# Attention's first loads in order of use, and the last stage's first operands loaded during attention

## What is computed

```python
proj = h @ w_in                                     # q, k, v, latent, indexer and gate columns
y_a = swa_sink_attention(qa, ka, va, sinks) @ w_o_a  # attention output: 512 columns per branch
y_b = dsa_mla_attention(qb, c_kv, qi, k_idx, w_idx, w_uk, w_uv, topk) @ w_o_b
mix = (sigmoid(g_a) * y_a + sigmoid(g_b) * y_b) @ w_out
h = layer_norm(ALPHA * h + mix, ln1_g, ln1_b)
ff = (silu(h @ w_ff_gate) * (h @ w_ff_up)) @ w_ff_down
return layer_norm(ALPHA * h + ff, ln2_g, ln2_b)
```

## Time and profile before

| | |
|---|---|
| three executions | 3710.90, 3723.59, 3720.97 us |
| their median | 3720.97 us |
| the profiled execution | 3723.26 us, its span 3721.0 us |
| granted PE clock, mean over the span | 0.979 of full |
| PE busy | 3484.1 us of the span (94%) |
| stages by first and last PE instruction | up to 1049.5; attention 1052.8 to 1990.2; last stage 2008.4 to the end |
| mean rate of the transfers | 126 GB/s |

### The profile page before, as it was taken

The page is one execution under the profiler, slowest core; times in us unless marked ns, Lnnn a source line. Parts: engine busy times, 40 slices in busy tenths (PEclk is TensorE's granted clock), DMA queues, the critical chain, the costliest instruction groups (busy, mean ns, idle before and its releaser), DMA issues. The chain is left out here.

```text
span 3721.0 us, 52571 instructions
## 1 busy us (share of the span) xinstructions
PE 3484.1 (94%) x17924; PEld 2896.5 (78%) x17924; DVE 2220.3 (60%) x3097; ACT 1923.8 (52%) x3592; POOL 1698.7 (46%) x1806
## 2 busy tenths in 40 slices
PE   6888999898989999999997998999999999999997
PEld 5776777677767888988996777778887888888786
DVE  5236888787623565666543665764556545555867
ACT  3223787788635798887553332343334333344443
POOL 5233443765311222222003665656665666554756
PEclk9999999999989999999998999999999999999998
DMA  8344323332221111100005445754545444365663
GB/s 272 129 125 109 101 88 124 124 89 74 83 70 51 40 42 35 35 16 19 23 11 181 152 167 180 242 188 141 183 142 188 160 142 150 123 249 191 235 227 132
DMA packets 338458, 468.44 MB, mean 126 GB/s; under 512 B 23184, under 2 KB 225120, under 8 KB 334992
## 3 DMA queue, kind: packets, MB, share of 16 engines
q1 hardware_dynamic: 310064, 387.47, 32.1%
q10 hardware_dynamic: 28128, 77.60, 5.7%
HBM read 311.21 MB, written 153.78 MB: 125 GB/s over the span
## 5 line engine op out<-in xcount | busy, mean ns | idle before, releaser
L2610 POOL TENSOR_TENSOR ff_rounded_ring<-ff_raw,ff_rounded_ring 128x512 fp32r<-128x512 f32 x264 | 383.4, 1464 | 292.0 <-ACT ff_rounded_ring L2757 289.4
L100 PE MATMUL ff_bank<-ff_rounded_pair,ff_rounded_ring 128*128 128x512 f32 x1232 | 482.9, 392 | 16.0 <-POOL ff_rounded_ring L2610 10.9
L101 PE MATMUL ff_bank<-ff_rounded_pair,ff_rounded_ring 128*128 128x512 f32 x1232 | 481.8, 391 | 0.0
L102 PE MATMUL ff_bank<-ff_rounded_pair,ff_rounded_ring 128*128 128x512 f32 x1232 | 481.6, 391 | 0.0
L1777 PE MATMUL at_ctx<-at_p_t,at_c_nat 128*128 128x128 f32 (+1 forms) x2432 | 344.5, 282 | 8.3 <-ACT at_ctx_t L1893 7.3
L1777 PEld LDWEIGHTS at_ctx<-at_p_t,at_c_nat 128*128 128x128 f32 (+1 forms) x2432 | 301.2, 191 | 35.6 <-ACT at_ctx_t L1893 13.2
L1887 ACT ACTIVATE at_p_t<-at_turn 128x512 f32<-128x512 f32 (+4 forms) x416 | 213.2, 544 | 204.9 <-PE at_turn L1754 174.9
L2615 POOL TENSOR_TENSOR ff_rounded_ring<-ff_raw,ff_rounded_ring 128x512 fp32r<-128x512 f32 x154 | 211.4, 1378 | 175.9 <-ACT ff_rounded_ring L2807 175.9
L3038 DVE TENSOR_TENSOR ff_rounded_a_ring<-ff_f_q,ff_rounded_a_ring 128x512 fp32r<-128x512 f32 x154 | 211.0, 1380 | 129.9 <-ACT ff_rounded_a_ring L2799 128.7
L100 PEld LDWEIGHTS ff_bank<-ff_rounded_pair,ff_rounded_ring 128*128 128x128 f32 x1232 | 232.7, 189 | 68.2 <-POOL ff_rounded_ring L2610 13.8
L102 PEld LDWEIGHTS ff_bank<-ff_rounded_pair,ff_rounded_ring 128*128 128x128 f32 x1232 | 232.7, 189 | 48.9
(11 more groups left out here) (401 smaller groups left out, 9075.5 us busy)
## 6 DMA issues: line engine op xcount, KB each, us to landing
f_kept<-ff_resid SPq DMA_DIRECT2D x154, 256.0 KB, 2.7
ff_f_q<-f_kept ACTq DMA_DIRECT2D x12, 2816.0 KB, 10.7
pj_raw<-in_w_in SPq DMA_DIRECT2D x58, 512.0 KB, 4.5
proj<-se_row SPq DMA_DIRECT2D x104, 256.0 KB, 2.2
ff_raw<-in_w_ff_gate SPq DMA_DIRECT2D x22, 1024.0 KB, 10.9
ff_raw<-in_w_ff_up SPq DMA_DIRECT2D x22, 1024.0 KB, 6.3
ff_raw<-down_comb SPq DMA_DIRECT2D x88, 256.0 KB, 2.7
ff_raw<-in_w_ff_down SPq DMA_DIRECT2D x66, 256.0 KB, 3.3
```

Of the source, the lines that this page charges most:

```text
L100: pe.matmul(out, lhs_lo, rhs_hi, start=start, stop=False, skip_group_check=goes_on)
L101: pe.matmul(out, lhs_hi, rhs_hi, start=False, stop=False, skip_group_check=goes_on)
L102: return pe.matmul(out, lhs_hi, rhs_lo, start=False, stop=stop, skip_group_check=goes_on)
L2610: pool.tensor_tensor(ring[:, step % RING, 1, :].rearrange("p (k c) -> p k c", c=P), f_operand(it, q, m), f32(ring[:, step % RING, 0, :]).r ...
```

## The change

It has three parts.

1. **Attention's list of loads (SP) is put in order of use.** Behind `qb` come the first keys, the distances of tile 0, the first three 128-row pieces of `c_nat` (`load_natural`), the distances of tile 1, the four small operands, the first window's operands, and then `wuv`, the other keys and the rest of `c_nat`. `c_nat` gets semaphores of its own (`nat_loaded`), waited for where PE first multiplies with it (step 0 and step 16), so that the logits wait for `c_hi` and `c_lo` alone. PE's wait for `w_loaded` moves from ahead of step 0 into step 1.
2. **Early loads.** Two buffers of 16 KB a partition, `early[0]` and `early[1]`, are placed at the far end of the memory, above a pad of 32 bytes. While attention runs, SP loads columns 0 to 511 of `w_o_a` and `w_o_b` into the first (behind the loads of tile 6) and the first branch's half of group 0's attention output into the upper half of the second (behind those of tile 7, with a wait for the stores of the first four tiles). The four `p_t` buffers of attention, which stood among its others, now lie in the other half of `early[1]`.
3. **The last stage uses them.** `w_o` is now held as two buffers by column (`early[0]`: columns 0 to 511; `w_o_second`: 512 to 1023) with both branches' rows in each, so rounding and subtracting a block take one instruction of 128x1024 each. `att` is `early[1]`. SP starts with the gates, then loads the second half of `w_o`; ACT loads only the second half of the first group's attention output. `ring` and `a_ring` lie where `early[0]` and `early[1]` were, two of three `raw_f` buffers lie in `att`, and the first two loads of feed-forward weights wait for `att_lo_ready` instead of the last block of `w_o`.

Every buffer of attention but `p_t` stands 8192 bytes lower than before and every one of the last stage but those named 16384 bytes lower or elsewhere by a multiple of 256. `early[0]`, `early[1]` (and so `p_t`, `att`, `ring`, `a_ring`) begin at a byte that leaves 192 when divided by 256; their predecessors began at one that leaves 128. The built program has 32 ACT and 32 POOL instructions of computation fewer, two waits of PE fewer, the same matmuls and the same DVE instructions.

```diff
+    def far(self, name, shape, dt=F32):
+        return self.enter_context(self.nc.sbuf_tensor(f"{self.tag}_{name}", shape, dt, side="right"))
...
-        p_t = [s.sb(f"p_t{u}", [P, 4, P]) for u in range(PT)]
+        p_t = [early[1][:, KT // 2 + u, :].rearrange("p (m c) -> p m c", m=4) for u in range(PT)]
...
+                first, first_rows = width(1), -(-width(1) // P)
+                load_keys(0, first, 0)
                 load_distances(0)
+                load_natural(0, first_rows, 0)
                 load_distances(1)
...
                 load_window(0)
                 load_values(0)
+                sp.dma_start(wuv[:, :, :], w_uv[0].rearrange("h r d -> r h d")).then_inc(w_loaded, 16)
+                load_keys(first, L, 1)
+                load_natural(first_rows, TILES, 1)
...
                     load_values(t + 1)
+                    if t == 5:
+                        for e, src in enumerate((w_o_a, w_o_b)):
+                            sp.dma_start(early[0][:, 4 * e:4 * e + 4, :], src.rearrange("(k p) c -> p k c", p=P)[:, :, 0:GROUP]).then_inc(early_loaded[0], 16)
+                    if t == 6:
+                        sp.wait_ge(attn_stored, 32 * TPG)
+                        sp.dma_start(early[1][:, 0:4, :], attn[0:512, 0:GROUP].rearrange("(k p) c -> p k c", p=P)).then_inc(early_loaded[1], 16)
...
-                        pe.wait_ge(c_loaded[t // 2], (64, 32)[t // 2])
+                        pe.wait_ge(c_loaded[t // 2], 32)
...
+                        if n in (0, 2 * HEADS):
+                            pe.wait_ge(nat_loaded[n // (2 * HEADS)], (16, 32)[n // (2 * HEADS)])
...
-                pe.wait_ge(w_loaded, 16 * 5)
                 for n in range(STEPS):
...
+                    if n == 1:
+                        pe.wait_ge(w_loaded, 16 * 5)
...
+        ring, a_ring = [s.far(name, [P, RING, 2, GROUP], F32R) for name in ("ring", "a_ring")]
...
+        raw_f = [att[:, 4 * u:4 * u + 4, :].rearrange("p k c -> p (k c)").rearrange("p (k c) -> p k c", c=2 * P) for u in range(2)]
...
-                        for u in range(2):
-                            sp.wait_ge(lo_ready[u], use1(NG - 1, KT - 2 + u) + 1)
+                        sp.wait_ge(att_lo_ready, KT * NG)
...
-                load_w_o(0)
                 load_gates(0, 0)
                 load_gates(0, 1)
+                load_w_o(0)
                 load_w_o(1)
...
-                load_w_o(2)
-                load_w_o(3)
...
-                        for d, src in block_parts(b):
-                            last = pool.tensor_tensor(as_k(w_lo[u])[:, d, :], src, as_k(f32(w_hi[u]))[:, d, :], ALU.subtract)
-                        last.then_inc(lo_ready[u], 1)
+                        pool.tensor_tensor(as_k(w_lo[u]), block_part(b), as_k(f32(w_hi[u])), ALU.subtract).then_inc(lo_ready[u], 1)
...
-                        if g == 0:
-                            act.wait_ge(w_o_loaded[b // 2], 32)
+                        if g == 0 and b < 4:
+                            act.wait_ge(early_loaded[0], 32)
+                        elif g == 0:
+                            act.wait_ge(w_o_loaded[b // 2 - 2], 32)
...
-                    for e in range(2):
+                    for e in range(0 if g else 1, 2):
                         act.dma_start(att[:, 4 * e:4 * e + 4, :], ...
...
+            kept.far("pad", [P, KT])
+            early = [first.far(f"half{u}", [P, KT, GROUP]) for u in range(2)]
```

77 lines of the change are left out of this document (37 added, 40 removed).

## The result

| | before | after |
|---|---|---|
| executions | 6: 3710.90 to 3723.59 us | 6: 3729.64 to 3746.27 us |
| median | 3716.72 us | 3740.11 us |
| profiled execution, its span | 3723.26, 3721.0 us | 3741.65, 3739.9 us |
| granted PE clock | 0.979 | 0.979 |

The ratio is 1.0065, with a 95% interval of 1.0053 to 1.0076: the kernel became slower by 23 us where 16 us of gain were forecast, and its time lies above the range of 3695 to 3715 us. Both savings that the forecast counted are there at their own places; two losses that it set at 0 are larger than both together.

What follows compares the result with a forecast made beforehand. PE was taken as the bound, busy 94% of the span, so only its waits at two stage starts could pay. Terms of -6.5 and -9.5 us, 16.0 off the 3721.0 us median, gave 3705 us, range 3695 to 3715.

Steps and rivals of the forecast that it cites:

- The start of attention: Up to step 0's transposes: waits for first keys and distances go, the clock stays full; -6.5 us, bounds -4.0 and -7.1.
- I take the upper end: At attention's start: PE stays at 2.4 GHz, with no idle stretch since its warm-up; 2.5 us saved, bounds 0 and 2.5.
- The clock falls elsewhere: Rival: a half-clock stretch like 1086 to 1096 comes once more (3710 us, chance 0.14) or vanishes (3700 us, 0.09).
- The loads during attention: Attention: three added 1 MB transfers make nobody wait; cost 0, without the slack up to 2 x 11.6 us once.
- The start of the last stage: PE's first product there comes 10.6 us sooner, 1.0 us is given back; -9.5 us, bounds -6.0 and -10.6.
- 32 ACT and 32 POOL instructions fewer lie beside a busy PE: 0: Rest of the last stage: fewer ACT and POOL instructions change nothing, as PE is busy there; 0 us.
- The addresses: I take 0 for it: `ring` and `a_ring` beginning 64 bytes past a multiple of 128 cost nothing, judged by transposes from `u_b`; 0 us.
- Slower: Rival: new places of `ring` and `a_ring` slow the products reading them; 3755 us at 4%; chance 0.05 beyond 2.2%.
- the signs for both starts: No waits 1063 to 1070, full clock 1070 to 1076, transposes near 1069.2; last stage's only PE wait 7 to 9 us.
- unchanged rows for L100 to L102: Sign of being right: these product rows stay as before; an L100 median above 395 ns would show it wrong.
- The last of the wrong signs: A start of either stage is sooner but the span's end is not: a later load or the clock took it back.

Runs made afterwards that it cites:

- e8: The kernel before with only attention's first loads put in order of use, with their own semaphores and waits; 3708.81 us, ratio to before 0.9996.
- e2: The changed kernel with POOL's subtraction of a block in two instructions of 128x512 instead of one; 3722.19 us, ratio to before 1.0025.
- e9: The changed kernel with a pad of 96 bytes and POOL's subtraction in four instructions of 128x256; 3696.6 us, ratio to before 0.9955.
- e6: The changed kernel with the last stage's near-side buffers, the pairs (moving operands) among them, moved by 64 bytes; 3716.76 us, ratio to before 1.0002.
- e1: The changed kernel with a pad of 96 bytes instead of 32, so far-end buffers begin at multiples of 128; 3716.48 us, ratio to before 1.001.
- e5: The changed kernel with a pad of 96 bytes and POOL's subtraction in two instructions of 128x512; 3699.61 us, ratio to before 0.9959.
- e13: e5 with attention's first loads in the order of the kernel before; 3700.95 us, ratio to before 0.9961.

## Why the prediction was wrong

- **The start of attention** (-6.5): right at its place, -7.4 in the profile. As a gain in the whole it was too much: 3.0 us in the mean of the traces, 1.6 in e8's time. The 4.0 us of waits are there (PE's idle time in attention is 3.8 us less in the mean, and less in every trace). The step that failed is "I take the upper end" of the clock's saving, 2.5 us: it is there from 1059 to 1063, but over the whole of attention PE's busy time scatters by 10 us with the granted clock, and nothing of it can be seen. The rival "The clock falls elsewhere" described this.
- **The loads during attention** (0): right, +0.4 us over 918.
- **The start of the last stage** (-9.5): right. PE starts 10.1 us sooner where 10.6 were worked out, and gives back 1.1 us in its wait for the second slice where 1.0 was taken. For `att`'s second half ACT waited 1.9 us, PE not at all.
- **"32 ACT and 32 POOL instructions fewer lie beside a busy PE: 0"** failed: +18 us. I counted the instructions that went, and not that the 32 left are twice as long. The row on which I rested, 82.6 of 83 us busy, ends at 2100, just where the first of the places with an idle PE begins: the window from 2098 shows 26.34 of 28 us. I had also cited the rule at issue, on the Trainium skill's page "SBUF — State Buffer", section "Who interferes with whom" (a VectorE instruction that needs the pair of ports shared with GpSimd waits for GpSimd's whole instruction), and applied it to two slices at the stage's start. The trace of the kernel before had the case to which it applied nine times in twelve: its scaling took 1284 ns at the least, for the first of each group, and 2305 in the median. With one POOL instruction twice as long, the scaling would wait for 2.4 us less POOL's head start instead of 1.3 us less it, 1.1 us more: 3.4 us, as measured. Twelve scalings took 16.4 us more of DVE's time (3 x 2.15 for the first of each group, which had been alone before, and 9 x 1.11). On PE, which is what counts, the trace of e2 is 18.5 us shorter here: 10.4 us less idle (22.5 against 32.9) and 8.1 less busy with the same matmuls (372.4 against 380.4, at 0.98 of the clock instead of 0.96). In the seven other traces with the single instruction PE's idle time is 31.8 to 36.2 us, in the other five with two it is 21.5 to 23.2, and in e9 with four 20.6. The share of the clock is less sure: busy times are 375.7 to 381.9 us with one instruction and 368.7 to 375.2 with two.
- **"The addresses: I take 0 for it"** failed: +21.7 us. The rival "Slower" named the products and the threshold, 2.2% for a slower kernel: the products took 2.6% more (5.9 of 227 ns), though only two thirds of them did. Its reason was near and not right: not the new places slow the products but their distance from the other operand's, which is why e6, with `ring` at the same new place, is fast, and why the down products of the kernel after did not slow. Its chance, 0.05, rested on the earlier trace rows, transposes of 128x128 from `u_b`. That was no evidence, for two reasons. Their moving operand `ident` leaves 128 when divided by 256, by the built program, and the three `u_b` leave 192, 0 and 64: no transpose had equal places to compare with. And matmuls of 128x128 don't show the effect. The products of 128x128 with `p_t` as the moving operand and `c_nat` as weights, where `p_t` moved by 64 bytes against `c_nat`, have a median of 275 ns in the kernel before, in the kernel after and in e1 alike.
- **What would show it**: the signs for both starts came true in the main, the granted clock from 1070 to 1076 (1.00) included. The transposes came still sooner than 1069.2, by the 5.6 us of the stage before and 0.9 us; PE had a wait of 0.6 us for ACT at 1063.6, in step 0 itself (0.5 before); and at the last stage a wait of 1.1 us came beside the one of 8.1. The sign "unchanged rows for L100 to L102" didn't: the median was 394 ns, 1 ns short of the 395 that I had set as the mark, which was too high a mark for 3696 matmuls. The last of the wrong signs, starts that are sooner and an end that is not, is what came.

Without the two steps the sum comes out: e5 has 3699.6 us where before had 3715.0 in the same comparison, 15.4 us less, against 16.0. That it comes so near is partly luck. The interval is 10 to 20 us, and the two terms do not come out so well one by one: e8 has 1.6 us (-2.2 to 4.8) for the start of attention where 6.5 were forecast, and e13 has 14 (9 to 20) for the last stage and the early loads where it was 9.5.
